# A two-layer hybrid decoder step on one core: front stages in one block, modulation in column strips, final norm inside the last projection

## The reference, cut to what matters

```python
def _rmsnorm(x, g):
    y = xf * lax.rsqrt(jnp.mean(xf * xf, axis=-1, keepdims=True) + NORM_EPS)
    return (y * g).astype(x.dtype)

def _modulation(c, w_ada, b_ada):
    shift, scale, gate = jnp.split(c @ w_ada + b_ada, 3, axis=-1)
...
    shift, scale, gate = _modulation(c, ada_w, ada_b)
    h = _rmsnorm(x, norm_g) * (1 + scale) + shift
    q, kv6, gl, z_a, x_b, z_b = _split(h @ w_in, L0_SIZES)
...
    y = jnp.concatenate([o_a * jax.nn.silu(z_a), o_b * jax.nn.silu(z_b)], axis=-1) @ w_out
    return x + gate * y, ...
```

## Time and profile before

| what | us |
|---|---|
| median of three runs | 2315.91 (2314.22 to 2325.44) |
| profiled execution, its own time | 2321.67 |
| its span, first to last instruction | 2319.9 |
| PE / DVE / ACT / POOL busy | 1865.5 / 1210.8 / 626.4 / 206.6 |
| first matmul of the first projection | at 123.67 |
| recurrence, from block to block | 396.3 to 485 |
| output projection of layer 0 | 948.4 to 1081.5 |
| output projection of layer 1 | 2164.7 to 2294.4 |
| final norm, to the end of the span | 2294.4 to 2319.9 |

### The profile page before, as it was taken

The page is one execution under the profiler, slowest core; times in us unless marked ns, Lnnn a source line. Parts: engine busy times, 40 slices in busy tenths (PEclk is TensorE's granted clock), DMA queues, the critical chain, the costliest instruction groups (busy, mean ns, idle before and its releaser), DMA issues. The chain is left out here.

```text
span 2319.9 us, 29122 instructions
## 1 busy us (share of the span) xinstructions
PE 1865.5 (80%) x11577; PEld 1283.2 (55%) x11577; DVE 1210.8 (52%) x2379; ACT 626.4 (27%) x1574; POOL 206.6 (9%) x190
## 2 busy tenths in 40 slices
PE   5589998969999667596899987978867667787595
PEld 2289998336666444384676644554542344444383
DVE  0231002757777652443223899946956998233443
ACT  0331121555666112002111000005633444222101
POOL 0033120000000531000011000000020000331000
PEclk9789999979999877598999999989987999898698
DMA  6321111400000554310111101100010000884301
GB/s 207 155 113 55 57 38 50 161 34 1 1 1 2 243 247 182 147 46 30 62 61 42 48 19 38 38 0 1 1 51 23 1 1 1 322 352 197 147 1 75
DMA packets 38450, 188.53 MB, mean 81 GB/s; under 512 B 8267, under 2 KB 8364, under 8 KB 21738
## 3 DMA queue, kind: packets, MB, share of 16 engines
q0 software_dynamic: 16912, 102.68, 11.3%
q1 hardware_dynamic: 21404, 83.98, 10.0%
HBM read 171.69 MB, written 19.12 MB: 82 GB/s over the span
## 5 line engine op out<-in xcount | busy, mean ns | idle before, releaser
L729 PE MATMUL banks<-hT,w_in 128*128 128x352 f32 x864 | 264.5, 465 | 39.9 <-DVE qdT L801 18.8
L729 PEld LDWEIGHTS banks<-hT,w_in 128*128 128x128 f32 x864 | 163.9, 192 | 138.5 <-DVE qdT L801 21.1
L2471 PE MATMUL banks<-w_out_parts,mix_parts 128*128 128x512 f32 (+1 forms) x864 | 204.8, 400 | 36.1 <-DVE w_out_parts L176 36.1
L2471 PEld LDWEIGHTS banks<-w_out_parts,mix_parts 128*128 128x128 f32 (+1 forms) x864 | 159.8, 186 | 83.5 <-DVE w_out_parts L176 40.4
L1304 ACT ACTIVATE nsa_p<-banks,nsa_negmax 128x512 f32<-128x512 f32 (+3 forms) x192 | 104.2, 557 | 94.0 <-DVE nsa_negmax L1223 94.0
L724 PE MATMUL banks<-hT_rest,w_in_high 128*128 128x352 f32 x384 | 124.0, 323 | 0.0
L724 PE MATMUL banks<-hT_high,w_in_high 128*128 128x352 f32 x384 | 124.0, 323 | 0.0
L724 PE MATMUL banks<-hT_high,w_in_rest 128*128 128x352 f32 x384 | 123.9, 323 | 0.0
L726 PE MATMUL banks<-w_in,hT 128*128 128x256 f32 (+3 forms) x576 | 118.9, 362 | 6.1 <-DMA w_in<-in_w_in 6.1
L1223 DVE TENSOR_REDUCE nsa_negmax<-banks 128x2 f32<-128x1024 f32 (+4 forms) x77 | 84.6, 1099 | 69.7 <-PE banks L1177 59.4
L853 ACT ACTIVATE mix<-banks 128x352 f32<-128x352 f32 x48 | 22.0, 465 | 348.4 <-PE banks L729 229.0
(11 more groups left out here) (525 smaller groups left out, 3566.4 us busy)
## 6 DMA issues: line engine op xcount, KB each, us to landing
w_in<-in_w_in SPq DMA_DIRECT2D x24, 1056.0 KB, 4.9
ada_w<-in_ada SPq DMA_DIRECT2D x24, 1024.0 KB, 4.9
w_out<-in_l_w_out SPq DMA_DIRECT2D x4, 2048.0 KB, 7.7
x_in<-in_x_prompt SPq DMA_DIRECT2D x1, 4096.0 KB, 15.0
nsa_ring<-in_state_l_win_kv POOLq DMA_DIRECT2D x8, 512.0 KB, 6.9
x_after<-in_x_prompt SPq DMA_DIRECT2D x1, 4096.0 KB, 17.8
x_mid<-x_after SPq DMA_DIRECT2D x8, 512.0 KB
x_after<-x_mid SPq DMA_DIRECT2D x1, 4096.0 KB, 17.9
```

What stands on the lines that cost most here:

```text
L729: last = pe.matmul(bank[:, 0:cn], w[:, j % slots, a, m * P:(m + 1) * P], k.hT[:, a, c0:c0 + cn], start=(a == 0), stop=(a == KT - 1))
L2471: last = pe.matmul(k.bank[u % 4][0:n, :], lhs, rhs, start=a == 0 and x == 0, stop=a == KT - 1 and x == 2)
```

## The change

Layer 0's front becomes one block, `front`: `x` is loaded right behind the constants, in two halves with a semaphore each, ahead of the modulation weights; the small loads move from SP's queue to POOL's; squares, root, scaling and transposes of a half run while the modulation pieces come in, and scale and shift are applied afterwards to the finished `hT`, five channel tiles on DVE and three on ACT. Only the 8 pieces of shift and scale are computed here; the 4 gate pieces go to the recurrence, which then has 16 pieces, four for a channel tile. `w_in`'s first two blocks are loaded in the same block, and for layer 1 in `normalise`. In `multiply` the operand `cT` is padded to 32 columns and the eight matmuls write four strips of 32 PSUM partitions in turn; the sum over the strips is taken by `turn`, now a product with `quarters` (128 x 9 ones at q % 32 = n), and for the gate by constants with a one in each strip. In the output projection the weights come in quarters, rounded by ACT, with DVE taking only the rest; mix tiles 0 and 1 are split first; the units begin (0,0), (0,1), (1,0), (1,1) (column half, row tile). In layer 1 the final norm's gain is spread at the beginning, and squares, root, scaling and store run per row tile behind the units.

```diff
     def multiply(self, pe, n):
...
-        o = self.banks[j % 2][0:NC, 0:WB]
+        o = self.banks[n % 2]
         for a in range(KT):
-            pe.matmul(o, k.cT[:, a, :], self.w[:, s, a, :], start=(a == 0), stop=False)
+            g = 32 * (a % 4)
+            pe.matmul(o[g:g + 32, 0:WB], k.cT[:, a, :], self.w[:, s, a, :], start=a < 4, stop=False, skip_group_check=True)
...
+def front(k):
...
+                for g in range(2):
+                    sp.dma_start(k.x[:, 4 * g:4 * g + 4, :], ...).then_inc(x_loaded[g], 16)
+                sp.dma_start(k.x[0:NS, RT - 1, :], ...).then_inc(x_loaded[2], 16)
+                m.load(sp)
+                for j in range(len(k.w0_loaded)):
+                    sp.dma_start(k.w0[:, j], ...).then_inc(k.w0_loaded[j], 16)
...
+                for a in range(5):
+                    dve.tensor_scalar(k.hT[:, a, 0:SEQ], k.hT[:, a, 0:SEQ], k.mod_as[0][:, a, 0:1], k.mod_bs[0][:, a, 0:1], ALU.mult, ALU.add)
...
-        m = Modulation(k, st, 1, 2, [k.bank[4], ...])
+        m = Modulation(k, st, 1, [*((0, j) for j in range(8, 12)), *((1, j) for j in range(12))], 2, [k.bank[4], ...])
...
-        units = [(h, r) for r in range(RT) for h in range(2)]
+        units = [(0, 0), (0, 1), (1, 0), (1, 1), *((h, r) for r in range(2, RT) for h in range(2))]
...
+                for h in range(2):
+                    for c in range(2):
+                        if h:
+                            sp.wait_ge(w_ready, c + 1)
+                        sp.dma_start(raw[:, quarter(c), :], ...).then_inc(loaded[h][c], 16)
...
+                    if layer == 1 and h == 1 and r >= 1:
+                        scale(r - 1)
+                if layer == 1:
+                    scale(RT - 1)
...
+                for h in range(2):
+                    for c in range(2):
+                        act.wait_ge(loaded[h][c], 16)
+                        act.activation(w[:, h, 0, quarter(c)], raw[:, quarter(c), :], ACT.Copy).then_inc(w_rounded, 1)
```

More of the change, by code:

```diff
@@ L219, in build @@
                         if layer == 0:
-                            k.h_high = k.sb(held, "hT_high", [P, KT, R], FR, side="right")
-                        normalise(k, layer)
+                            k.w0_rest = k.under("w_in_rest", [P, 2, KT, WIN_B], FR, side="right")
+                            k.w0 = k.sb(held, "w_in0", [P, 2, KT, WIN_B], side="right")
+                            k.w0_loaded = [k.sem(held, f"w_loaded0_{i}") for i in range(2)]
+                            front(k)
+                        else:
+                            k.w1 = k.sb(held, "w_in1", [P, 2, KT, WIN_B], side="right")
+                            k.w1_loaded = [k.sem(held, f"w_loaded1_{i}") for i in range(2)]
+                            normalise(k, layer)
                         x_stack.close()
@@ L242, in build @@
                 k.give_back_semaphores()
-        final_norm(k)
         x_stack.close()
@@ new lines, in _ @@
+                m.copy_vectors(act)
+                for n in range(3):
+                    m.copy(act, n)
+                for g in range(2):
+                    for a in range(1, KT, 2):
+                        u = g * KT + a
+                        act.wait_ge(turned, u + 1)
+                        act.activation(k.hT[:, a, g * 512:(g + 1) * 512], k.bank[2 + u % 4][:, :], ACT.Copy).then_inc(read_act, 1)
+                    m.copy(act, 3 + 2 * g)
+                    m.copy(act, 4 + 2 * g)
@@ L583, in project @@
     with ExitStack() as st:
+        w = k.w0 if layer == 0 else k.w1
+        w_rest = k.w0_rest
         if parted:
-            w_rest = k.under("w_in_rest", [P, slots, KT, WIN_B], FR)
-        w = k.sb(st, f"w_in{layer}", [P, slots, KT, WIN_B])
+            k.h_high = k.sb(st, "hT_high", [P, KT, R], FR)
         stage = k.sb(st, f"kv_rows{layer}", [P, stages, WB])
-        w_loaded = [k.sem(st, f"w_loaded{layer}_{i}") for i in range(slots)]
+        w_loaded = k.w0_loaded if layer == 0 else k.w1_loaded
         full = [k.sem(st, f"proj_full{layer}_{i}") for i in range(4)]
@@ L654, in _ @@
             def _(sp):
-                for j in range(len(blocks)):
+                for j in range(slots, len(blocks)):
                     if j >= slots:
@@ L2430, in output_projection @@
         mix_ready = k.sem(st, f"mix_split{layer}")
-        units = [(h, r) for r in range(RT) for h in range(2)]
+        units = [(0, 0), (0, 1), (1, 0), (1, 1), *((h, r) for r in range(2, RT) for h in range(2))]
+        units_to = [max(u for u, x in enumerate(units) if x[1] == r) + 1 for r in range(RT)]
+        quarter = lambda c: slice(c * KT // 2, (c + 1) * KT // 2)
+        if layer == 1:
+            g = k.sb(st, "final_g", [P, D])
+            grow = k.sb(st, "final_g_row", [1, D])
+            junk = k.sb(st, "final_junk", [P, D])
+            ss = k.sb(st, "final_ss", [P, RT])
+            g_loaded = k.sem(st, "final_loaded")
+            squared = k.sem(st, "final_squared")
+            mean = k.sem(st, "final_mean")
+            root = k.sem(st, "final_root")
+            done = k.sem(st, "final_done")
         with nc.Block() as block:
```

403 lines of the change are left out of this document (230 added, 173 removed).

## The result

The changed kernel takes 2246.69 us against 2315.3 us of the kernel before in the same session, a ratio of 0.969 [0.9654, 0.9726]. It is faster, as forecast, but by 69 us instead of 103, and 8.7 us above the range of 2200 to 2238. One of its four executions, at a granted clock of 0.715, took 2499.43 us; the ratio is that of the other three. The profiled execution has a span of 2243.3 us.

What follows compares the result with a forecast made beforehand. The prediction saw PE bound overall, but chains of waits between stages in the places changed. Terms -57.7 - 2 - 6 - 12 - 7.5 - 18 sum to -103, bringing the median from 2315.91 to 2213 us, range 2200 to 2238.

Steps and rivals of the forecast that it cites:

- Front, -57.7: Start to first projection matmul: from 123.7 to 66 us, range -48 to -61.
- the step on DMA: Front: loads flow at 411 GB/s plus 2.3 us latency, so the third modulation piece lands at about 25.5 us.
- `turn` and `finish` stay: Front: last copy to the end of mod_a keeps its 3.9 us, reaching 49.3 us.
- Recurrence, -2: Recurrence with four modulation pieces per channel tile: -2 us, range -6 to +5, taken between full and half clock.
- The gain of 5.5: Recurrence at full clock: three tile periods give -5.5 us, each bounded near 15 instead of 16.8.
- The first rival: Low clock in front and recurrence: first matmul at 76, recurrence +5, sum -86, total 2230 us; chance 0.14.
- The second rival: Modulation pieces: strips do not overlap, a piece stays at 4.07 us; sum -73, total 2243 us; chance 0.06.
- the 0.45: Strip pieces: tiling-mode drain priced at one undisturbed matmul, 0.226 us, for each of two changes per piece.
- Third and fourth rival: Third: final norm's waits hold last projection, 2227, chance 0.04; fourth: low clock slows first projection, up to +130, chance 0.01.
- weights ahead: Layer 1's projection: loading w_in during the norm removes the 6.15 us wait; -6 us, range -5 to -7.
- the output projections: Layer 0: shorter waits for weights, -12 us (-9 to -13.5); layer 1: also the gain first, -7.5 (-5 to -9.5).
- the final norm: After the last product: 27.2 us shrink to 9, earlier tiles hidden under PE; -18 us, range -16 to -19.

Runs made afterwards that it cites:

- The three runs on the loads: Changed kernel with all twelve small loads, SP's later large loads, or only page numbers held until x landed: first projection matmul 71.9, 82.5, 72.9 us against 81.9.
- the runs that moved it: Changed kernel with small loads behind x and front's turn in parts: first matmul 69.3 us; changed kernel with recurrence's turn in the last tile's gap: recurrence 87.8 us.
- Filling: Changed kernel plus 11 unused matmuls between second and third modulation piece of each recurrence tile: recurrence 82.2 us against 95.1.
- moved turn: Changed kernel with layer 1's turn put between second and third piece of the recurrence's last tile: recurrence 87.8 us against 95.1.
- combined: Changed kernel with small loads behind x, filling in three tiles, turn in the fourth: 2223.33 us; with front's turn in parts too: 2216.86 us.
- the better run: Changed kernel with small loads behind x, filling in three tiles, turn in the fourth, front's turn in parts: 2216.86 us, 0.957 of the kernel before.
- the copies ahead: ScalarE copies a tile's first two pieces before waiting for the factor: recurrence 92.5 us on the changed kernel; on the combined version with 7 filling matmuls, 84.5 us, 2221.17 total.

## Why the prediction was wrong, point by point

**Front, -57.7 against -41.7: the step on DMA failed.** I let the bytes in SP's queue flow at the 411 GB/s of one window of the earlier trace rows and gave the small loads no price, because they move almost no bytes. They were part of the change, in the diff, moved from a stretch in which they ran alone to one in which some 8 MB are queued. The three runs on the loads give 10.1 of the 16 us, the turn 2.5 (below), and 3.3 are the third piece's late start: the nine squares, which I had hidden under the loads, keep ScalarE from the copies that it waits for. The price of the small loads stood in the trace of before as 8 us in which DMA moved 1 GB/s.

**"`turn` and `finish` stay": false.** Strips leave four partial sums, and the turn that adds them is another operation: 32 full matmul instructions, 4.51 and 7.00 us, instead of 16 transposes in 1.16 and 1.15. On the path this was 2.5 us in the front and 7.3 us behind the recurrence, by the runs that moved it.

**Recurrence, -2 against +15.8: I stood in the middle where the trace pointed to one end.** The prediction counted two periods, 15 us at full clock and 18.5 at the low level, noted that TensorE would be busy for some 60% like the stretch that stood at 0.50, and took the mean. The low level came, and the period was 20.0. The 18.5 was also too small by its own terms: slow gates keep the root waiting too, so 11.8, 1.85 more for the gates (5.7 less 3.85), a copy of 0.4 and 2 x 2.7 make 19.5. The root ended 13.9 us behind the start of its tile's gates. Of the 15.8 the three periods are 6.8 (59.7 less 52.9), and 9.0 lie behind the last gates, where 5.85 are the turn and I had counted nothing. Filling (-12.9) and moved turn (-7.3) cover the 15.8 and more; combined they give 77.7 to 80.5, about the 79.3 of before. The gain of 5.5 that I had forecast at full clock was not reached: in the better run the three periods are 49.5 us instead of 52.9. Part of this are the loads, which two slots were to bring in time: with the copies ahead the third piece waits 3.2 to 3.5 us for its load.

**The first rival had the mechanism in the recurrence, and too little of it.** It put the recurrence at +5 and the front's first matmul at 76, both by the clock. The low level came in the recurrence, at +15.8 with the turn. In the front the granted clock reads 1.00 from 40 to 60 us; yet the 16 matmuls of the third piece take 1.94 us, as at 0.50 in the recurrence, and the 32 transposes behind it 5.45, the next 32 only 3.71. From the third piece on that is 3 us and not the rival's 10. The kernel before has the same at a reading of 1.00, 6.27 us for its first piece's 16 matmuls and 3.62 for the next; so early in an execution the reading alone does not show the speed. The rival's 2230 is 17 us short; the loads (10.1) and the turn (2.5 and 7.3) stood in no rival.

**The second rival fell.** The strips do overlap: 0.067 us a matmul, 0.227 without. A whole piece of 18 instructions takes 1.55 us at full clock, 0.15 more than worked out from line 1879. The Trainium skill, "TensorEngine Tiling (Array Packing)", section "Tiling Modes", says that a change of mode drains TensorE; the trace leaves at most 0.15 us a piece for it, not the 0.45 that I had set against it.

**Third and fourth rival did not come.** The last projection is not held by the final norm's waits (its stretch came out 2 us better than forecast), and the long first projection takes 285.9 us against 285.1.

**Right by its own steps:** weights ahead (shown by undoing it), the output projections and the final norm. The latter two rest on the rows above alone; no run took them apart.

## What to carry to other kernels

Before moving small loads beside large ones, look at how long they run alone and at what rate, not at their bytes: 8 KB of page numbers cost 9 us. Work taken from TensorE is won only if the clock does not fall for what follows; where the bound is elsewhere, put late work into the gap (here the turn, which then cost nothing but did not hold the clock) or even empty matmuls (which did), and read the granted clock behind it. When a trick leaves partial results, price the step that adds them up as a new operation.

## What was not expected of the hardware

Eight loads of 1 KB held back the first half of a 4 MB load in another queue by 9 us (12 with the four lambda loads), with DMA at 99 to 179 GB/s instead of 416. Eleven matmuls a tile that compute nothing made a stage 12.9 us faster; the turn in the same place, busy throughout by the trace, left the clock at 0.50. And three times the work on TensorE cost a tile 3 us: at a granted clock of 1.00 and busy throughout it needed 23.4 us, at 0.67 and with a third of the work 20.0.
